# Seven block products for the two branch projections of a hybrid state-space, attention and expert layer

## What is computed

```python
branch_a = y_ssd @ w_ssm_out            # (640, 2048) @ (2048, 1024), y_ssd after its rmsnorm
branch_b = o @ w_attn_out               # (640, 1024) @ (1024, 1024), o is the attention output
gates = jax.nn.sigmoid(g.astype(f32)).reshape(b, T, N_BRANCHES, D_MODEL)
merged = (gates[:, :, 0] * branch_a.astype(f32)
          + gates[:, :, 1] * branch_b.astype(f32)).astype(x.dtype)
return x + merged @ w_o, k, v, ki, conv_new, ssm_new
```

## Time and profile before

| | |
|---|---|
| median of 3 runs | 1472.26 us (1472.23 to 1473.79) |
| profiled execution | 1473.76 us |
| its span | 1471.9 us |
| TensorE matmul busy | 1343.3 us (91%) |
| VectorE busy | 790.8 us (54%) |
| ScalarE busy | 494.3 us (34%) |
| DMA | 247.45 MB, mean 168 GB/s |

### The profile page before, as it was taken

The page is one execution under the profiler, slowest core; times in us unless marked ns, Lnnn a source line. Parts: engine busy times, 40 slices in busy tenths (PEclk is TensorE's granted clock), DMA queues, the critical chain, the costliest instruction groups (busy, mean ns, idle before and its releaser), DMA issues. The chain is left out here.

```text
span 1471.9 us, 19541 instructions
## 1 busy us (share of the span) xinstructions
PE 1343.3 (91%) x7218; PEld 904.4 (61%) x7218; DVE 790.8 (54%) x1707; ACT 494.3 (34%) x1155; POOL 234.3 (16%) x334
## 2 busy tenths in 40 slices
PE   7999999899999999998988999999999979878880
PEld 5555766676766767775667677777765545544440
DVE  4259888898898899897745511111014533111105
ACT  3153134655565575426755320000002211121112
POOL 3000000220321231223700000000000023222210
PEclk9999999999999999998999999999999989998995
DMA  8422424435435434435047433213036389999965
GB/s 272 124 43 46 143 78 142 128 118 142 142 94 157 127 119 132 125 123 130 2 108 153 186 86 123 50 63 140 27 119 270 143 331 413 416 414 415 414 245 221
DMA packets 148689, 247.45 MB, mean 168 GB/s; under 512 B 40053, under 2 KB 107365, under 8 KB 139669
## 3 DMA queue, kind: packets, MB, share of 16 engines
q1 hardware_dynamic: 137524, 215.10, 43.8%
q0 software_dynamic: 11072, 31.12, 6.0%
HBM read 216.50 MB, written 36.88 MB: 172 GB/s over the span
## 5 line engine op out<-in xcount | busy, mean ns | idle before, releaser
L672 PE MATMUL psum<-hT,wring 128*128 128x320 f32 x1024 | 290.4, 436 | 2.6 <-ACT wring L648 2.2
L672 PEld LDWEIGHTS psum<-hT,wring 128*128 128x128 f32 x1024 | 193.3, 191 | 86.2 <-ACT wring L648 5.4
L672 PE MATMUL psum<-wring 128*128 128x320 f32 x768 | 217.4, 433 | 0.0
L672 PEld LDWEIGHTS psum<-wring 128*128 128x128 f32 x768 | 145.7, 190 | 61.4 <-ACT wring L648 0.9
L1444 PE MATMUL psum<-ident,arena 128*128 128x128 f32 (+3 forms) x950 | 138.9, 286 | 27.6 <-ACT arena L1942 11.7
L1444 PEld LDWEIGHTS psum<-ident,arena 128*128 128x128 f32 (+3 forms) x950 | 106.2, 144 | 80.7 <-issue 53.5
L1440 PE MATMUL psum<-arena,wring 128*128 128x320 f32 x512 | 138.1, 431 | 0.0
L1440 PEld LDWEIGHTS psum<-arena,wring 128*128 128x128 f32 x512 | 96.6, 189 | 41.2
L648 ACT ACTIVATE wring<-psum 128x320 f32<-128x320 f32 (+2 forms) x140 | 50.2, 381 | 170.1 <-PE psum L672 169.5
L1942 ACT ACTIVATE arena<-psum 128x512 f32<-128x512 f32 (+8 forms) x155 | 73.2, 521 | 70.3 <-PE psum L1444 43.8
L2088 ACT ACTIVATE arena<-arena 128x1024 f32<-128x1024 f32 x5 | 5.3, 1058 | 261.2 <-DVE arena L2714 261.2
(11 more groups left out here) (350 smaller groups left out, 1998.3 us busy)
## 6 DMA issues: line engine op xcount, KB each, us to landing
wring<-in_w SPq DMA_DIRECT2D x32, 1024.0 KB
arena<-in_w SPq DMA_DIRECT2D x54, 512.0 KB
wring<-in_w_in SPq DMA_DIRECT2D x25, 1024.0 KB, 5.5
oT<-in_w SPq DMA_DIRECT2D x12, 1024.0 KB
arena<-a_rows SPq DMA_DIRECT2D x20, 512.0 KB, 3.9
hT<-in_w SPq DMA_DIRECT2D x10, 1024.0 KB
arena<-in_w SPq DMA_DIRECT2D x10, 1024.0 KB
arena<-in_state_ssm SPq DMA_DIRECT2D x16, 512.0 KB, 7.4
```

Of the source, the lines that this page charges most:

```text
L672: ins = nc.tensor.matmul(o[:, 0:TH], wt[:, k, :], rows[:, k, :], start=n in (1, 5, 2) and k == 0, stop=k == 3, skip_group_check=True)
```

## The change

`LATE` names eight new pairs: four of branch b and then four of branch a, where the halves n alternated between b and a before. Each is a pair of two channel blocks, made in seven products by `dense_late`. For branch a each product runs over two chunks of weights and rows, eight matmuls.

- Weight sums lie in place of blocks that are not needed any more: sum 3 overwrites the top right block, sum 2 the top left one once product 1 is done, sum 4 the low left one once product 2 is done. Sum 1 has three homes in turn (`sum1_homes`: columns of `kvtm` and `hT`).
- Row sums of the attention output and of the state output are made once for all four pairs (`sum_late_rows`), in free columns of `arena`, `wring`, `kvtm` and `oT`; sum 3 overwrites a block of the rows themselves.
- ScalarE stages products 1, 6, 5 and 7. VectorE's `gated` adds a block and then multiplies it by its gate.
- Weights have other homes: both attention chunks in slots 0 and 1, the first two state chunks in slot 2 and in `hT`, the third in `oT` once attention's products are done, the fourth in slot 1, `w_o` in slot 2 and in `hT`. Experts 2 and 3 swap their slots of `wring`.

```diff
+LATE = [(_w, _n, _i) for _w in ("b", "a") for _n in range(2) for _i in range(2)]
+PAIRS_ALL = DENSE + LATE
...
-    for n in range(2):
-        for what in ("b", "a"):
-            for c in range(4):
-                for h in range(2):
-                    b.add((what, n, c, h), any8)
+    for i, key in enumerate(LATE):
+        plan_pair(b, key, (3, 4, 5) if i % 2 else (0, 6, 7))
...
-        ring.add(("wao", n), 0, ("b", n, 3, 1), [
+        ring.add(("wao", n), n, ("b", 1, 1, 4), [
...
+    for n in range(2):
         for c in range(2):
-            ring.add(("wso", n, c), 1 + c, ("a", n, 3, 1),
+            ring.add(("wso", n, c), c if n else 2 + c, ("a", n, 1, 4),
                      [(lambda s: s[:, :, :], wso_r[:, 8 * c:8 * c + 8, 512 * n:512 * n + 512])])
...
-        ring.add(("wo", n), 3 * n, ("x1", NT - 1, 1), [(lambda s: s[:, :, :], wo_r[:, :, 512 * n:512 * n + 512])])
+        ring.add(("wo", n), 2 + n, ("x1", NT - 1, 1), [(lambda s: s[:, :, :], wo_r[:, :, 512 * n:512 * n + 512])])
...
+        def dense_late(pe, key):
+
+            what = key[0]
+            for n in SEVEN:
+                o = claim(pe, key + (n,))
+                weights_sum = {5: 1, 6: 2, 3: 4, 7: 3}
+                rows_sum = {5: 1, 6: 2, 4: 4, 7: 3}
+                for c in chunks_of(key):
+                    if n == 1:
+                        wait_chunk(pe, late_chunk(key, c))
+                        if what == "a":
+                            pe.wait_ge(S["y_back"], 16)
+                    if n in weights_sum:
+                        pe.wait_ge(S["sums_ready"], SUM_AT[("w", key, c, weights_sum[n])])
+                    if n in rows_sum and key[1:] == (0, 0):
+                        pe.wait_ge(S["sums_ready"], SUM_AT[("rows", what, c, rows_sum[n])])
...
+                    for k in range(4):
...
+                        ins = nc.tensor.matmul(o[:, 0:TH], wt[:, k, :], rows, start=n in (1, 5, 2) and k == 0 and c == 0,
+                                               stop=k == 3 and c == len(chunks_of(key)) - 1, skip_group_check=True)
+                filled(ins, key + (n,))
...
+        def sum_second(dve, key):
+
+            wait_full(dve, key + (1,))
+            for c in chunks_of(key):
+                tl, tr, bl, br = late_weights(key, c)
+                dve.wait_ge(S["sums_ready"], SUM_AT[("w", key, c, 3)])
+                summed(nc.vector.tensor_tensor(tl, sum1(key, c), tl, ALU.subtract), ("w", key, c, 2))
...
-            gates_act(act, late[-1], fn)
+            for at, key in enumerate(LATE):
+                for n in HELD:
+                    pair_staged(act, key, n)
+                    if at == 0 and n == 1:
+                        gates_act(act, late[-1], fn)
...
+                    key = (what, 1, i)
+                    pair_added(dve, key, (0, 0))
+                    if key == DENSE[-1]:
+                        sum_first(dve, LATE[0])
+                    pair_added(dve, key, (1, 1))
+                    pair_added(dve, key, (0, 1))
...
+                    if key == ("ga", 1, 1):
+                        sum_late_rows(dve, "b", 0, 1)
+                        sum_late_rows(dve, "b", 0, 2)
+                    if key == ("gb", 1, 0):
+                        sum_late_rows(dve, "b", 0, 4)
+                        sum_late_rows(dve, "b", 0, 3)
...
+            for at, key in enumerate(LATE):
+                what, m, i = key
+                if what == "b":
+                    dve.wait_ge(S["gates_ready"], 4 * m + 3 + i)
+                sum_second(dve, key)
+                gated(key, (0, 0))
+                sum_fourth(dve, key)
+                if key in (("b", 1, 0), ("b", 1, 1)):
+                    if i == 0:
+                        dve.wait_ge(S["y_back"], 16)
+                        wait_full(dve, ("b", 0, 1, 4))
+                    for r in (1, 2, 3):
+                        sum_late_rows(dve, "a", i, r)
+                if key == ("a", 0, 0):
+                    wait_full(dve, ("b", 1, 1, 4))
+                    for c in range(2):
+                        sum_late_rows(dve, "a", c, 4)
+                gated(key, (1, 1))
+                if at + 1 < len(LATE):
+                    sum_first(dve, LATE[at + 1])
+                gated(key, (0, 1))
+                gated(key, (1, 0))
+                if at < 2:
+                    scaled_gates(at)
+                if what == "a":
+                    wait_read(dve, key + (4,))
+                    for j in range(2 * i, 2 * i + 2):
+                        row = mrg[:, 4 * m + j, :]
+                        tt_(row, row, gate_tile("gb", m, j), ALU.add).then_inc(S["m_ready"], 1)
```

More of the change, by code:

```diff
@@ L127, with chunks_of, late_sums @@
 SUMMED = {key: 4 * i + (4 if i else 0) for i, key in enumerate(DENSE)}
+LATE = [(_w, _n, _i) for _w in ("b", "a") for _n in range(2) for _i in range(2)]
+PAIRS_ALL = DENSE + LATE
+def chunks_of(key):
+    return range(2 if key[0] == "a" else 1)
+def late_sums():
+    order = [("rows", "b", 0, r) for r in (1, 2, 4, 3)]
+    for c in (1, 3):
+        order.append(("w", LATE[0], 0, c))
+    for at, key in enumerate(LATE):
+        order += [("w", key, c, 2) for c in chunks_of(key)]
+        order += [("w", key, c, 4) for c in chunks_of(key)]
+        if key in (("b", 1, 0), ("b", 1, 1)):
+            order += [("rows", "a", key[2], r) for r in (1, 2, 3)]
+        if key == ("a", 0, 0):
+            order += [("rows", "a", c, 4) for c in range(2)]
+        if at + 1 < len(LATE):
+            order += [("w", LATE[at + 1], c, r) for c in chunks_of(LATE[at + 1]) for r in (1, 3)]
+    return order
+LATE_ORDER = late_sums()
+SUM_AT = {what: 4 * len(DENSE) + 4 + i + 1 for i, what in enumerate(LATE_ORDER)}
 def plan_banks():
@@ L577, in stage @@
         def stage(key, n):
[L579 removed]
+            if key[0] in ("a", "b") or key[0] in ("ga", "gb") and key[1]:
                 return [(stage_late[:, HELD.index(n), :], 0, TH)]
@@ L697, in sum_rows, with late_chunk, late_weights, sum1 @@
             tt_(top_r, low_r, top_r, ALU.subtract).then_inc(S["sums_ready"], 1)
+        def late_chunk(key, c):
+            return ("wao", key[1]) if key[0] == "b" else ("wso", key[1], c)
+        def late_weights(key, c):
+            w, at = slot(late_chunk(key, c)), 256 * key[2]
+            return [w[:, 4 * i:4 * i + 4, at + P * j:at + P * (j + 1)] for i in range(2) for j in range(2)]
+        def sum1(key, c):
+            return sum1_homes[sum1_turns.index((key, c)) % 3].rearrange("p (k n) -> p k n", k=4)
@@ L1580, in _ @@
                     dense(pe, (what, 1, i))
[L1581 to L1596, removed]
+            for key in LATE:
+                dense_late(pe, key)
             ws = [wait_chunk(pe, ("wo", n)) for n in range(2)]
@@ L2687, in branch_a, with gated @@
-            def branch_a(m):
+                    if key == ("ga", 1, 1):
[4 more added lines that the diff above has]
+                        sum_late_rows(dve, "b", 0, 3)
+            def gated(key, block):
+                what, m, i = key
+                a, h = block
+                j = 2 * i + a
+                half = slice(h * TH, (h + 1) * TH)
+                gate_ = gate_tile("g" + what, m, j)[:, half]
+                out = gate_ if what == "b" else mrg[:, 4 * m + j, half]
+                if block == (1, 0):
+                    wait_full(dve, key + (4,))
+                    release(tt_(out, bank(key + (4,))[:, 0:TH], gate_, ALU.mult), key + (4,))
+                    return
+                whole = rr[:, 0:TH]
+                if block == (1, 1):
+                    wait_read(dve, key + (5,))
+                    wait_read(dve, key + (7,))
+                    link(tt_(whole, held(key, 7, 0, TH), held(key, 5, 0, TH), ALU.add))
+                else:
+                    n, first = (2, 1) if h == 0 else (3, 6)
+                    wait_full(dve, key + (n,))
+                    wait_read(dve, key + (first,))
+                    release(tt_(whole, bank(key + (n,))[:, 0:TH], held(key, first, 0, TH), ALU.add), key + (n,))
+                    wait_read(dve, key + (n,))
+                link(tt_(out, whole, gate_, ALU.mult))
```

108 lines of the change are left out of this document (79 added, 29 removed).

## The result

The changed kernel takes **1447.96 us** (median of 4 runs, 1447.39 to 1448.78); the kernel before, run beside it, 1472.43. The ratio is 0.9831, with a 95% interval of 0.9815 to 0.9847: 24.5 us less. The forecast was 1447.6. The profiled execution took 1447.95 us with a span of 1446.3. In all that follows one execution alone stood apart: one of the 13 of the kernel before that ran beside "before again" took 2327.90 us at a mean granted clock of 0.56, where the others have 0.96, and it is left out of that median.

What follows compares the result with a forecast made beforehand. In the branch stage only the number of TensorE matmuls was taken to set the time. -25.8 + 0.75 + 0.4 = -24.7 us, from a profiled 1473.76 to 1449.1, the run median 1.5 lower: 1447.6 us, range 1445.5 to 1452.0.

Steps and rivals of the forecast that it cites:

- Matmuls: Branch stage on TensorE: 96 fewer matmul records at a pitch of 0.2692 us each, -25.8 us.
- The seam in front: Last gate pair to first new pair: TensorE waits for ScalarE to drain PSUM bank 0, +0.75 us.
- The gate scaling: VectorE's 128x2560 scaling behind the first two pairs delays weight sum 2 for product 6: 0.2 us twice, +0.4.
- The other sums: Remaining weight sums, row sums and gating steps on VectorE in the branch stage all meet their deadlines: 0 us.
- The queues: Attention, state and output weight loads for the branch stage arrive before they are wanted: 0 us.
- The seam behind: After the last product VectorE merges two rows, so later loads start 0.8 us later against TensorE; slack covers it: 0.
- Costly changeovers: Rival: seven later changeovers, or one in-pair sum per pair, cost 0.89 us each, 6.2 us, giving 1453.8; chance 0.08.
- A swallowed shift: Rival: the expert stage ends when it did, its weights setting the end, giving 1472; half eaten, 1460; chance 0.05.
- The clock: Rival: small idle times in the branch stage drop TensorE to 1.2 GHz; at one fifth, 11 us slower, 1483; chance 0.02.
- rival C: Branch stage: small idle times between products lower TensorE's granted clock; at one fifth, 11 us slower, 1483; chance 0.02.
- The upper bound of the costs: Forecast's upper end from unknown waits in the branch stage, 0.9 and 0.9 twice: about 1449.3 us.

Runs made afterwards that it cites:

- before again: The unchanged kernel from before the change, profiled and timed once more: 1472.89 us, against 1473.65 for the kernel before run beside it.
- filler: Changed kernel plus twelve unneeded VectorE steps at each of five seams from the third pair on, 31 us of work: 1453.79 us.
- without cover: Changed kernel with TensorE's late-pair products reordered to 1, 6, 2, 5, 7, 3, 4, so product 6 directly follows product 1: 1459.07 us.

## Why the prediction was right, step by step

- **Matmuls, -25.8.** Right. 96 records at 0.2692 us. It rests on reading the pitch from starts rather than the mean duration; put back as a dose they cost 25.6 (with 0.26 covered), and a third of them 8.3.
- **The seam in front, +0.75.** Measured +0.79, and it vanishes with other banks. The 0.1 set behind the drain was right in size only: the drain ends at 883.12, TensorE starts 0.05 later and then loses 0.10 in the restart, which the sum didn't have.
- **The gate scaling, +0.4.** The mechanism was right and the size too large: 0.13 us each, 0.26 in all. The sum was ready 4.21 us into the pair, as worked out; product 6 starts 0.15 us behind that, so 0.05 late, and the restart adds 0.08. The 0.2 that I took had no working behind it. It is the smallest term and still showed in two starts.
- **The other sums, 0.** Right (79.8 us of VectorE in the stage, 83 forecast), and not because VectorE is under half busy: without its product in between, each sum 2 costs 1.1 us or more. The walk through one pair of each kind was the step that carried this. It also gave the filler's price seam by seam.
- **The queues, 0.** Right in the sum, wrong in a margin. The first chunk was wanted by VectorE at 872.4 and came at 881.01, not 879; with the sums behind it, VectorE was through by 883.2, and product 5 wanted the first of them at 889.7. TensorE's own use of the chunk had about 1.5 us left, not three.
- **The seam behind, 0.** Right: the loads go 0.74 us later against TensorE, and the first expert product keeps its distance of 100.4 us.
- **The rivals.** Costly changeovers: of seven later ones two cost 0.13 and five nothing. A swallowed shift: none. The stretch behind was 1.15 us shorter in the change's profile, which is scatter, as the second profile of before shows.
- **The clock.** It was 1.00, even without cover. But one argument for that was a misreading: the clock of this case does not fall only where TensorE is idle half the time. The kernel before has this at 199.88 us (TensorE), and then this stretch:

```profile
199.88 0.41 PE L1182 MATMUL psum<-arena,ones 128*128 128x32 f32 x2 [1.56 <-ACT arena L1796]
```

```profile
202.00:206.00 4.00, 4.00 (x13) 2.73 (x12) 3.86 (x8) 1.15 (x5) 0.00 (x0) 0.50 0.00 0
```

Behind matmuls of 32 columns and one idle time of 1.56 us the clock stands at 0.50, the 1.2 GHz level, while TensorE is busy for all of 4 us. What brought it down there no run tests. So what speaks against rival C is the gate pairs and the runs, above all the one without cover.

The upper bound of the costs is a little off, too: 0.9 us three times gives 1449.2, not 1449.3.

That the total came within 0.4 us owes something to luck: identical code ahead of the stage ended between 881.4 and 885.1 us in these profiles. What can be vouched for is the stage.

## What to carry to other kernels

Where an engine is busy without a gap, price a removed instruction by the distance between starts, not by its duration. Where a cheap engine then has to feed it, don't ask how busy that engine is: list for each operand the moment it can be made and the moment it is wanted, and put one unrelated product between. Look at the first and the last use of a resource at the edges of a rewritten stage (here PSUM bank 0), since a rotation that is sound inside may meet its neighbour's last use there.

## What the runs showed that was not expected

- A wait can cost time without an idle entry. Product 6 behind the scaling started 0.05 us late and its run took 0.08 more, and the profile lists no idle time for TensorE there, since the modelled end of the run before covers 0.16 us. The wait at the seam is listed with 0.53 us and cost 0.79.
- Restarting costs 0.08 to 0.10 us beyond the wait, whether the wait was 0.05 or 3.5 us long.
- Between profiles the time up to the branch stage differed by 3.7 us for the same code, and the stretch behind it by 1.9 (382.97 and 381.08 in the two of before), more than both of the small terms that were at stake. The stage itself repeated to 0.01 us.
